# First loads of a stage issued in the stage before it, and cache moves spread over the tiles of a merge

## The reference: what is computed

```
h = x + W_out( sum_b sigmoid(G_b n) * P_b(branch_b(n)) ),   n = RMSNorm(x)
y = h + PEER(RMSNorm(h))

wts = softmax(stack(lses), axis=0)                     # 3 groups of dilated attention
od  = sum(wts[..., None] * stack(outs), axis=0)        # mixed per head
merged = gt[:, :, 0] * br_gla + gt[:, :, 1] * br_dil + gt[:, :, 2] * br_mem
h = x + merged @ w_out
```

## Time and profile before

| | us |
|---|---|
| median of 3 runs | 4730.08 (4729.22 to 4731.23) |
| the profiled execution's own time | 4724.34 |
| its span, first to last instruction | 4722.7 |

### The profile page before, as it was taken

The page is one execution under the profiler, slowest core; times in us unless marked ns, Lnnn a source line. Parts: engine busy times, 40 slices in busy tenths (PEclk is TensorE's granted clock), DMA queues, the critical chain, the costliest instruction groups (busy, mean ns, idle before and its releaser), DMA issues.

```text
span 4722.7 us, 55427 instructions
## 1 busy us (share of the span) xinstructions
PE 4178.8 (88%) x18639; PEld 2490.7 (53%) x18639; DVE 2463.3 (52%) x5405; ACT 1745.3 (37%) x4663; POOL 1538.0 (33%) x1403
## 2 busy tenths in 40 slices
PE   7999999997677987889898898898898888988987
PEld 6888888886545753444344343443443443444331
DVE  2111111114743743466666666666666666666664
ACT  2111111114523653244444444444444444444443
POOL 0000000002524522044444444444444444444443
PEclk9999999998788998899999999999999999999999
DMA  8899898883597747499999999999999999999998
GB/s 287 282 325 319 302 326 281 292 315 120 167 354 251 225 141 252 177 412 421 421 420 414 418 414 415 415 415 415 413 411 419 416 411 417 416 413 411 412 410 362
DMA packets 319837, 1642.22 MB, mean 348 GB/s; under 512 B 45065, under 2 KB 88297, under 8 KB 177658
## 3 DMA queue, kind: packets, MB, share of 16 engines
q0 software_dynamic: 164016, 1167.79, 60.4%
q1 hardware_dynamic: 119938, 249.55, 15.5%
q10 hardware_dynamic: 35648, 222.04, 14.0%
HBM read 1550.47 MB, written 318.03 MB: 396 GB/s over the span
## 4 chain that ended last, share of the span: by engine, by line
DMA 38%; PE 12%; issue 4%; ACT 4%; DVE 1%; POOL 0%; DVEq 0%; POOLq 0%; ACTq 0%; SPq 0%; PEldq 0%
DMA ex_rows<-scratch_uv,ex_E 38%; PE ex_ps_y L2804 9%; ACT ex_diag L2506 1%; PE ex_ps_q L2752 1%; ACT ex_w L2498 1%; ACT ex_gel L2494 1%; PE ex_ps_t L2717 1%; ACT L2494 0%; ACT L2489 0%; PE ex_ps_y L2798 0%; DVE ex_dots L2651 0%; DVE ex_rows L2651 0%; POOL ex_rows L2437 0%; ACT ex_ex L2489 0%; PE ex_ps_q L2765 0%
## 5 line engine op out<-in xcount | busy, mean ns | idle before, releaser
L2804 PE MATMUL ex_ps_y<-ex_rows,ex_diag 128*128 128x512 f32 (+1 forms) x4224 | 2030.9, 614 | 311.4 <-ACT ex_diag L2506 288.4
L2651 DVE CUSTOM_DVE_ANT_0 ex_rows<-ex_rows,ex_n2u 128x1024 f32<-128x1024 f32 x1056 | 1294.4, 1226 | 911.9 <-DMA ex_rows<-scratch_uv,ex_E 903.5
L2437 POOL DMA_INDIRECT ex_rows<-scratch_uv,ex_E x1056 | 1207.4, 1143 | 1577.4 <-PE ex_ps_y L2804 1436.1
L2804 PEld LDWEIGHTS ex_ps_y<-ex_rows,ex_diag 128*128 128x128 f32 (+1 forms) x4224 | 739.2, 189 | 1451.0 <-ACT ex_diag L2506 794.0
L412 PE MATMUL pj_ps<-pj_w_hi,pj_nT 128*128 128x470 f32 x3072 | 912.4, 377 | 3.9 <-DVE pj_w_lo L248 2.7
L2494 ACT ACTIVATE ex_gel<-ex_dots 128x1 f32<-128x1 f32 x1056 | 214.3, 203 | 1430.4 <-DVE ex_dots L2651 1429.2
L412 PEld LDWEIGHTS pj_ps<-pj_w_hi,pj_nT 128*128 128x128 f32 x3072 | 579.3, 189 | 86.0 <-issue 8.2
L412 PE MATMUL pj_ps<-pj_w_lo,pj_nT 128*128 128x470 f32 x1536 | 577.5, 376 | 0.0
L2506 ACT ACTIVATE ex_diag<-ex_ident,ex_w 128x128 f32<-128x128 f32 x1024 | 411.1, 401 | 33.5
L276 DVE COPY pj_zo<-pj_ps 128x470 f32<-128x470 f32 x96 | 61.3, 645 | 694.2 <-PE pj_ps L412 462.3
L276 ACT COPY pj_zo<-pj_ps 128x470 f32<-128x470 f32 x96 | 51.9, 553 | 802.5 <-PE pj_ps L412 476.2
(11 more groups left out here) (372 smaller groups left out, 3625.5 us busy)
## 6 DMA issues: line engine op xcount, KB each, us to landing
pj_w<-in_w_in POOLq DMA_DIRECT2D x24, 1880.0 KB, 17.8
scratch_z<-pj_zo SPq DMA_DIRECT2D x192, 235.0 KB, 11.6
scratch_uv<-in_peer_u ACTq DMA_DIRECT2D x8, 4096.0 KB, 25.3
scratch_uv<-in_peer_v ACTq DMA_DIRECT2D x8, 4096.0 KB, 42.8
scratch_uv<-in_peer_u ACTq DMA_DIRECT2D x4, 8192.0 KB, 41.7
scratch_uv<-in_peer_v ACTq DMA_DIRECT2D x4, 8192.0 KB, 73.3
out_dk_s<-in_cache_dil_k ACTq DMA_DIRECT2D x8, 4088.0 KB, 43.3
out_dv_s<-in_cache_dil_v ACTq DMA_DIRECT2D x8, 4088.0 KB, 54.9
```

Of the source, the lines that this page charges most:

```text
L2437: pool.indirect_dma_start(out=rows[:, p % SLOTS, :], out_offset=None, in_=d["uv"], in_offset=bass.IndirectOffsetOnAxis(ap=E[:, turn % 4, k ...
L2651: nc.vector.tensor_tensor_reduce(out=row, in0=row, in1=n2u[:, tile % 2], scale=1.0, scalar=0.0, op0=ALU.mult, op1=ALU.add, accum_out=dots[ ...
L2804: last = nc.tensor.matmul(y[0:n, 512 * c:512 * c + 512], diag[:, p % DIAGS, 0:n], rows[:, p % SLOTS, D + 512 * c:D + 512 * c + 512], start ...
```

## The change

Three parts.

1. A stage's first loads are issued in the stage before. `merge_early` allocates, in `attend`, the buffers of `lse`, `od3` and the rest of `a` for even tiles; after the last `store_o`, `attend` loads tile 0 into them. `experts_early` allocates, in `merge`, the buffers for the ident, iota, head 0 of `wq`, `g2`, `n2u`, `h` and `yo` of `experts`; `merge` fills them in its turns 3 to 6.
2. The 13 moves go from POOL to SP, two in each turn t from 0 to 5 and one in turn 6.
3. The raw keys land in `n2u[:, 1]` and `yo`, which are idle then, and no longer in row buffer 7; POOL's gather no longer waits for the keys' transposes, and the load of tile 1 into `n2u` does.

```diff
@@ attend, SP, after the last store_o
+                if n == LAST - 1:
+                    for i in range(2):
+                        after(sp, o_stored[i], ASK)
+                    sp.dma_start(merged.lse[:], d["lse"][:, 0:P, :].rearrange("g t h -> t g h")).then_inc(merged.b_in, 16)
+                    sp.dma_start(merged.od[:], d["od"][:, 0:P, :].rearrange("g t n -> t g n")).then_inc(merged.b_in, 16)
+                    sp.dma_start(merged.a[:, 512:1024], d["acts"][0:P, 1536:2048]).then_inc(merged.b_in, 16)
@@ new
+def merge_early(nc, d):
+    d["hold_mg"] = ExitStack()
+    sb = lambda n, s: d["hold_mg"].enter_context(nc.sbuf_tensor("mg_" + n, s, mybir.dt.float32))
+    d["mg_in"] = FirstMerged(lse=sb("lse_even", [P, NG, H]), od=sb("od3_even", [P, NG, 512]), a=sb("a_even", [P, D]), b_in=nc.alloc_semaphore("mg_b_in0"))
+    return d["mg_in"]
+def experts_early(nc, d):
+    sb = lambda n, s: held.enter_context(nc.sbuf_tensor("ex_" + n, s, mybir.dt.float32, side="right"))
+    d["ex_in"] = ExpertsFirst(held=held, ident=sb("ident", [P, P]), iota=sb("iota", [P, TOPK]), wq0=sb("wq0", [P, KD, 256]), g2=sb("g2", [P, D]),
+                              n2u=sb("n2u", [P, 2, D]), h=sb("h", [P, D]), yo=sb("yo", [P, D]), ident_in=sem("ex_ident_in"),
...
@@ merge, SP
-            for t in range(2):
-                load_a(t)
-                load_gate(t)
+            load_gate(0)
+            load_a(1)
+            load_gate(1)
             for t in range(N):
                 if t + 2 < N:
                     load_a(t + 2)
+                for dst, src in moves[2 * t:2 * t + 2]:
+                    sp.dma_start(dst, src).then_inc(moved, 16)
                 sp.wait_ge(added, NPRD * (t + 1))
                 sp.dma_start(d["h"][rows(t), :], m[0:width(t), t % 2]).then_inc(stored[t % 2], 16)
                 if t + 2 < N:
                     load_gate(t + 2)
+                if t == 3:
+                    sp.dma_start(early.ident[:], d["ident"]).then_inc(early.ident_in, 16)
+                    sp.dma_start(early.h[:], d["x"][0][rows(0), :]).then_inc(early.x_in, 16)
+                    sp.wait_ge(stored[0], 16)
+                    sp.dma_start(early.n2u[:, 0], d["h"][rows(0), :]).then_inc(early.m_in[0], 16)
+                if t == 4:
+                    sp.dma_start(early.g2[:], d["ln2_g"].partition_broadcast(P)).then_inc(early.consts_in, 16)
+                    sp.dma_start(early.iota[:], d["iota"]).then_inc(early.consts_in, 16)
+                    sp.dma_start(early.wq0[:], wq_dram[:, :, 0:256]).then_inc(early.consts_in, 16)
+                if t == 5:
+                    for g in range(PH):
+                        sp.dma_start(early.n2u[:, 1, g * P:(g + 1) * P], d["peer_keys"][g // 2, g % 2]).then_inc(early.keys_in, 16)
+                if t == 6:
+                    for g in range(PH, 2 * PH):
+                        sp.dma_start(early.yo[:, (g - PH) * P:(g - PH + 1) * P], d["peer_keys"][g // 2, g % 2]).then_inc(early.keys_in, 16)
+            sp.wait_ge(moved, 16 * len(moves))
@@ merge, POOL
-                if t == 1:
-                    for dst, src in moves:
-                        pool.dma_start(dst, src).then_inc(moved, 16)
-            pool.wait_ge(moved, 16 * len(moves))
@@ experts, SP
+                else:
+                    sp.wait_ge(keys_t, 2)
                 sp.dma_start(n2u[0:width(tile), tile % 2], d["h"][tokens(tile), :]).then_inc(m_in[tile % 2], 16)
...
-            sp.dma_start(ident[:], d["ident"]).then_inc(ident_in, 16)
-            load_m(0)
-            load_x(0)
-            sp.dma_start(g2[:], d["ln2_g"].partition_broadcast(P)).then_inc(consts_in, 16)
-            sp.dma_start(iota[:], d["iota"]).then_inc(consts_in, 16)
-            sp.dma_start(wq[:, :, 0:256], wq_dram[:, :, 0:256]).then_inc(consts_in, 16)
-            for g in range(2 * PH):
-                sp.dma_start(rows[:, SLOTS - 1, g * P:(g + 1) * P], d["peer_keys"][g // 2, g % 2]).then_inc(keys_in, 16)
-            sp.dma_start(wq[:, :, 256:], wq_dram[:, :, 256:]).then_inc(wq_in, 16)
+            sp.dma_start(wq[:], d["peer_wq"].rearrange("(k p) n -> p k n", p=P)[:, :, 256:]).then_inc(wq_in, 16)
@@ experts, POOL
-                    if p == SLOTS - 1:
-                        pool.wait_ge(keys_t, 2)
```

More of the change, by code:

```diff
@@ L2092, in _ @@
                     last.then_inc(v_used.sem, 1)
+@dataclass
+class FirstMerged:
+    lse: object
+    od: object
+    a: object
+    b_in: object
+@dataclass
+class ExpertsFirst:
+    held: object
+    ident: object
+    iota: object
+    wq0: object
+    g2: object
+    n2u: object
+    h: object
+    yo: object
+    ident_in: object
+    consts_in: object
+    keys_in: object
+    x_in: object
+    m_in: object
+def merge_early(nc, d):
+    from concourse import mybir
+    from contextlib import ExitStack
+    d["hold_mg"] = ExitStack()
[3 more added lines that the diff above has]
+def experts_early(nc, d):
+    from concourse import mybir
+    from contextlib import ExitStack
+    held = ExitStack()
+    sb = lambda n, s: held.enter_context(nc.sbuf_tensor("ex_" + n, s, mybir.dt.float32, side="right"))
+    sem = nc.alloc_semaphore
+    d["ex_in"] = ExpertsFirst(held=held, ident=sb("ident", [P, P]), iota=sb("iota", [P, TOPK]), wq0=sb("wq0", [P, KD, 256]), g2=sb("g2", [P, D]),
+                              n2u=sb("n2u", [P, 2, D]), h=sb("h", [P, D]), yo=sb("yo", [P, D]), ident_in=sem("ex_ident_in"),
+                              consts_in=sem("ex_consts_in"), keys_in=sem("ex_keys_in"), x_in=sem("ex_x_in"),
+                              m_in=[sem(f"ex_m_in{i}") for i in range(2)])
+    return d["ex_in"]
 def merge(nc, d):
@@ L2182, in _ @@
                            .rearrange("(b t) n -> b t n", b=DEC_B))]
+            wq_dram = d["peer_wq"].rearrange("(k p) n -> p k n", p=P)
+            load_gate(0)
+            load_a(1)
+            load_gate(1)
+            for t in range(N):
+                if t + 2 < N:
+                    load_a(t + 2)
+                for dst, src in moves[2 * t:2 * t + 2]:
+                    sp.dma_start(dst, src).then_inc(moved, 16)
+                sp.wait_ge(added, NPRD * (t + 1))
+                sp.dma_start(d["h"][rows(t), :], m[0:width(t), t % 2]).then_inc(stored[t % 2], 16)
+                if t + 2 < N:
+                    load_gate(t + 2)
+                if t == 3:
[14 more added lines that the diff above has]
+            sp.wait_ge(moved, 16 * len(moves))
+            sp.wait_ge(stored[0], 16 * ((N + 1) // 2))
+            sp.wait_ge(stored[1], 16 * (N // 2))
+        @block.gpsimd
+        def _(pool):
             for t in range(NT):
@@ L2728, in _, with head_weights @@
                 for k in range(8):
-                    last = nc.tensor.transpose(ps_y[:, g, k * P:(k + 1) * P], rows[:, SLOTS - 1, (8 * g + k) * P:(8 * g + k + 1) * P], ident[:])
+                    last = nc.tensor.transpose(ps_y[:, g, k * P:(k + 1) * P], (n2u[:, 1], yo[:])[g][:, k * P:(k + 1) * P], ident[:])
                 last.then_inc(keys_t, 1)
             pe.wait_ge(keys_out, 2)
+            def head_weights(head, k):
+                return wq0[:, k] if head == 0 else wq[:, k, (head - 1) * 256:head * 256]
             def turn_rows(turn):
```

80 lines of the change are left out of this document (37 added, 43 removed).

## The result

| | before | changed |
|---|---|---|
| median, us | 4730.65 (4 runs, 4729.22 to 4731.43) | 4677.01 (4 runs, 4671.15 to 4682.89) |
| ratio | | 0.9886 (0.9875 to 0.9898) |
| profiled execution, us (span) | 4724.34 (4722.7) | 4671.15 (4669.5) |
| first gather, us from the start | 2006.92 | 1995.71 |
| first gather to the end of the span | 2715.8 | 2673.8 |

The change gains 53.6 us, where I had forecast 14.5 and a range that ended at 4706. About 11 us of it lie ahead of the first gather. The other 42 lie behind it, in code that the change hardly touches.

The account below looks back on a forecast made before the run. It took the DMA of gathered expert rows as the bound, its length fixed, so only an earlier first gather counts: 4.9 + 11.2 + 3.9 - 5.5 = 14.5 us, median 4715.6, stated as 4715.5, range 4706 to 4723.5.

Parts of the forecast that it names:

- The start of merge, 4.9: Attend to merge: DVE starts 6.4 us earlier without waiting for loads, less 1.5 for attend's delayed last store; net 4.9 earlier.
- Rival D: Border of attend and merge: it doesn't open, 4.9 becomes 2, time 4718.5; chance 0.58 together with the forecast.
- Tile 3, 11.2: Merge, tile 3: with the moves off POOL and spread out, the whole stall goes, 11.2 us gained.
- Tiles 6 and 7, -5.5: Merge: moves in SP's queue delay loads behind them, giving back 5.5 us, within 0 to 12.
- step two: Merge, after the store of tile 4: `load_a(7)` comes 3.0 us late behind the queue's backlog and PE waits.
- Step three: Merge, after the store of tile 5: the gates of tile 7 land 2.5 us late.
- rival B: Merge: the stall returns almost whole at tiles 6 and 7, 12 us, border delay 2.8; time 4723.4, chance 0.14.
- the count of the queue in order: Merge, SP's queue: loads behind a move wait for all of it; 5.5 us given back at tiles 6 and 7.
- even sharing: Merge: moves and loads share the DMA engines evenly; tile 7's gates come at 15.9, not 16.5; 4.9 us instead of 5.5.
- Rival A: Merge: no congestion comes back, copies run at the gather's rate; gain 20.0 us, time 4710.1, chance 0.22.
- C: Merge: each 2.1 MB move holds SP's queue m us, stalls m - 3.4 and m - 3.9; 4760 at 25.5; chance 0.05.
- The start of experts, -3.9: Start of experts: PE begins with the stage, at 1956.0 and not 1959.93, 3.9 us earlier.

Follow-up runs that it names:

- e1: The kernel before with 192 unused bytes per partition ahead of the row buffers, which then start on a multiple of 256: 4691.69 us, ratio 0.9925.
- e2: The kernel before with the 192 unused bytes behind the row buffers, which stay 64 past a multiple of 256: 4729.67 us, ratio 1.0004.
- e8: e7 with tile 0's three loads issued two steps earlier in attend: 4666.78 us, ratio 0.9866.
- e4: The changed kernel with the 13 moves back on POOL's queue: 4684.60 us, ratio 0.9907.
- e3: The changed kernel with 64 unused bytes ahead of the row buffers, which then start 64 past a multiple of 256: 4715.87 us, ratio 0.9973.
- e7: The changed kernel with the two 2.1 MB moves issued in experts behind the load of `wq`, not in merge: 4672.69 us, ratio 0.9875.
- e9: The changed kernel run again without any edit: 4677.11 us, ratio 0.9884.

## Why the prediction was wrong, step by step

**The step that failed** is the first: "I take the time from the first gather at 2006.92 to the end as fixed in length". It was shortened by 42 us (38 to 42 by the other profiles). "The change touches nothing there but one wait long passed" was true of the instructions, and I had looked at them alone. The diff takes three buffers, 8768 bytes, from the allocation ahead of `ex_rows`, and so moves the target of 1056 gathers from 64 past a multiple of 256 to a multiple of 256. e1 and e2 show that this place alone is worth 37.7 us. The same slip made "the engines are full, 421 GB/s at a share of 1.01" a ceiling: it was the rate at that placement. No rival had it either. I had named as refuting me a gather changed by more than 2 us, and that is what came.

**The start of merge, 4.9: 3.5 measured.** That DVE's wait goes was right (0.03 us behind SP). The term that was mis-sized is the delay of attend's last store: I took 1.5 from bounds of 0 and 2.8, and it is 2.8 (6.08 against 3.24), confirmed by e8, which takes 2.7 of it away. That this is just the upper bound is chance, for the rate behind the bound didn't hold. The loads began 1.8 us ahead of the store (1789.43 and 1791.20), so a part of them was through by then; but from 1789.5 to 1795.5 the DMA engines moved 241 GB/s and not the 370 that I took from a tile of merge, and only 111 from 1790.5 to 1792.0. In the slow part, 1790.4 to 1791.8, 416 of 497 packets were under 512 bytes. Of the three loads `lse` alone has such short rows (4 floats), so it is the likely cause; no run leaves it out. Rival D doesn't hold: the border opened.

**Tile 3, 11.2: 11.2 measured.** The stores stand 14.62 apart, and e4 brings the stall back with the moves alone.

**Tiles 6 and 7, -5.5: -7.0 measured** (-4.5 to -5.6 in the four other profiles, so the size was right), and of my two steps one holds. Step two, `load_a(7)` late and PE waiting, was 3.0 and measured 3.86 (2.49 to 3.75 in the others). Step three had the gates of tile 7 late by 2.5 and PE held by them. The gates were late, but PE never stood for them: its 3.0 us (1.7 to 1.8 in the others) are the low clock. I had argued against rival B that a wait of about 3 us "leaves PE idle for less than the 4 us after which the clock was seen to fall"; after 3.86 us the next transposes were already at the lower level, and that turned a wait of 3.9 into a loss of 6.9. A shorter wait was no safer. This is tile 7 of e3:

```profile
1912.46 1.06 PE L2357 MATMUL mg_ps_a<-mg_ident,mg_a_odd 128*128 128x128 f32 x8 [2.49 <-issue]
...
1913.00:1914.00 1.00, 1.00 (x6) 0.66 (x5) 1.00 (x2) 0.39 (x1) 0.00 (x0) 0.70 1.04 430
```

PE stood for 2.49 us and did the transposes at the full clock, and then, busy again, fell to the lower level all the same (0.70 in the microsecond from 1913, 0.50 in the next two). The near agreement of the size, 2.5 against 3.0, is chance. Since e7 takes both away with the copies, the count of the queue in order fits for the load. So does even sharing, which differed in step three alone, and nothing here decides between them. Rival A (nothing comes back) falls, and B with its 12 us too. C falls as well: with its own first step, m - 3.4 = 3.86, a move holds the queue for m = 7.3 us (5.9 to 7.2 by the waits of the others), near my 6.4 and far from its 25.5.

**The start of experts, -3.9: -3.6 measured.** PE began 0.36 us after SP.

**Not foreseen, small:** -0.6 us and -2.2 us where I had 0. In the second the 32 matmuls at the low clock took 15.40 us in place of 16.87. The shorter idle time ahead (5.09 us, 8.68 before) doesn't explain it by itself: after 4.88 us in e4 they took 16.69, after 4.93 in e7 16.09. What differs in the rows is when the full clock came back, near 1956.8 and so 2.9 us into the matmuls, where before it was near 1968.8 and 5.8 us into them (my estimate from stretches of 1 us at 0.60 and 0.61); what sets that moment stays open.

Shown by runs: the place of the rows, the moves, the border. Open for the gather: why a start off the boundary costs 1.4 to 1.8% and not 3.1%; why 32 costs 6 to 11 us more than 64 or 128; and whether it is the write into SBUF itself or the way in which the gather's transfers are made up for such an address, which the traces don't tell apart.

## What to carry to other kernels

When a diff moves an allocation, write down the start address of every buffer that large transfers fill, before and after, and not only the order of the instructions: here 64 bytes weighed three times as much as all the rescheduling. Where a profile says that the DMA engines are full, read the GB/s beside it and try the target on a multiple of 256 bytes before taking the rate for a limit. Loads for the next stage were free two steps ahead of the last store of a stage, and cost 2.7 us directly in front of it; big copies belong in a stretch whose DMA share is low and whose queue nothing urgent follows.

## What was unexpected of the hardware

- 8 KB rows gathered into SBUF: 422 GB/s with the target on a multiple of 256 bytes (seven profiles of five kernels, 2673.4 to 2675.3 us from the first of 1056 gathers of 128 rows to the end), 415 to 416 at 64 or 128 bytes past one (2711.2 to 2715.8), 414 at 32 past (2721.9). The DMA share reads 1.01 in all.
- One issue on SP held the engine for 9.11 us while its queue was backed up by 2 MB copies and tile loads, where a store's issue takes 0.33. In e9 it was 9.80, and in e7, without the two 2 MB copies, the same issue still took 4.36. All that stood behind it on SP was bound for the same queue.
- The granted clock of PE fell from 2.4 to 1.2 GHz within an idle time of 3.86 us, so that this wait cost 6.9. In e9 a wait of 3.75 cost 5.6, and in e3 the clock fell after a wait of 2.49 us, when PE was at work again. Two stretches of 1 us of the changed kernel inside that wait, which began at 1910.07 - 3.86 = 1906.21:

```profile
1908.00:1909.00 1.00, 0.00 (x0) 0.00 (x0) 0.45 (x1) 0.00 (x0) 0.52 (x1) 1.00 1.04 408
1909.00:1910.00 1.00, 0.00 (x0) 0.00 (x0) 0.97 (x3) 0.00 (x0) 0.00 (x0) 0.51 1.16 444
```

  The clock is full until 1909 and low from there, before PE resumes. At the end of merge in the kernel before it had fallen some 4 us after PE's last matmul.
- 1.05 MB of loads directly ahead of a store put the store's landing back by 2.4 to 3.2 us (4.4 to 5.1 after its issue in seven profiles, 1.9 to 2.0 in three without them ahead), although they were issued up to 1.8 us ahead of it. The DMA engines moved 241 GB/s meanwhile, and 111 in the 1.5 us with the many short packets.
